# A one-core streaming encoder layer: softmax scores kept with their sign turned, softmax outputs ahead of older results, a bank of its own for turned v and y, and g_pre as one row spread by a product

## What is computed

```
proj = u @ w_in                      -> q, k, v of three attention branches
A: 4 heads, two maps each, T5 bias, causal by chunks of 64;
   w = softmax(map 0) - lam * softmax(map 1);  o = rmsnorm(w @ v, subln_g) * 0.8
B: 8 query heads over 2 shared k/v heads, a band of 2 chunks, T5 bias,
   and a sink term in the softmax's sum
C: 8 heads, a band of 9 chunks, relative bias
mixed = sum over branches of sigmoid(u @ w_gate + b_gate) * (y @ w_proj)
h = x + rmsnorm(mixed @ w_out, g_post_mix)
h = h + rmsnorm(conv_ffn(rmsnorm(h, g_pre_ffn)), g_post_ffn)
```

## Time and profile before

| | us |
|---|---|
| median of 3 runs (range) | 900.63 (898.75 to 901.16) |
| the profiled execution | 900.81 |
| its span, first to last instruction | 899.0 |
| TensorE busy | 875.3 |
| weight loads busy | 737.0 |
| GpSimd, VectorE, ScalarE busy | 455.3, 406.1, 397.4 |

### The profile page before, as it was taken

The page is one execution under the profiler, slowest core; times in us unless marked ns, Lnnn a source line. Parts: engine busy times, 40 slices in busy tenths (PEclk is TensorE's granted clock), DMA queues, the critical chain, the costliest instruction groups (busy, mean ns, idle before and its releaser), DMA issues.

```text
span 899.0 us, 13197 instructions
## 1 busy us (share of the span) xinstructions
PE 875.3 (97%) x4327; PEld 737.0 (82%) x4327; DVE 406.1 (45%) x889; ACT 397.4 (44%) x700; POOL 455.3 (51%) x622
## 2 busy tenths in 40 slices
PE   7999999999999999999999999999999999999997
PEld 6887888888888887888888889888888888888886
DVE  5678776666556652223222175444444444300004
ACT  5466566666655645333332245444444444311112
POOL 4453433324433327667766665555555555555551
PEclk9999999999999999999999999999999999999999
DMA  7442132332222212323335512333333332322202
GB/s 228 135 118 68 50 93 72 91 93 77 59 70 77 60 47 88 112 86 102 102 108 179 185 34 83 111 102 103 94 93 93 93 103 105 119 94 94 94 24 94
DMA packets 132141, 86.14 MB, mean 96 GB/s; under 512 B 6822, under 2 KB 121454, under 8 KB 132098
## 3 DMA queue, kind: packets, MB, share of 16 engines
q1 hardware_dynamic: 131050, 81.86, 30.4%
q10 hardware_dynamic: 1048, 3.72, 1.2%
HBM read 83.42 MB, written 2.14 MB: 95 GB/s over the span
## 4 chain that ended last, share of the span: by engine, by line
PE 86%; DVE 6%; ACT 3%; POOL 2%; issue 1%; DMA 1%; DVEq 0%; SPq 0%; POOLq 0%; ACTq 0%
PE banks L1237 27%; PE banks L1239 27%; PE banks L1238 27%; PE banks L1381 2%; POOL ring_lo L527 1%; PE banks L1310 1%; PE banks L1311 1%; DMA wide<-in_g_pre_mix_dram 1%; DVE scratch L1037 1%; PE banks L1256 1%; DVE pages L959 1%; DVE scratch L1066 1%; ACT pages L638 1%; DVE pages L954 0%; DVE pages L1000 0%
## 5 line engine op out<-in xcount | busy, mean ns | idle before, releaser
L527 POOL TENSOR_TENSOR ring_lo<-ring_raw,ring_hi 128x256 fp32r<-128x256 f32 x568 | 429.0, 789 | 394.3 <-ACT ring_hi L630 394.2
L1237 PE MATMUL banks<-u_hi,ring_hi 128*128 128x512 f32 (+1 forms) x800 | 309.8, 387 | 2.3 <-POOL ring_lo L527 1.7
L1239 PE MATMUL banks<-u_hi,ring_lo 128*128 128x512 f32 (+1 forms) x800 | 305.1, 381 | 0.0
L1238 PE MATMUL banks<-u_lo,ring_hi 128*128 128x512 f32 (+1 forms) x800 | 304.6, 381 | 0.0
L630 ACT CAST ring_hi<-ring_raw 128x1024 fp32r<-128x1024 f32 x142 | 147.8, 1043 | 134.6 <-PE banks L1239 126.3
L1237 PEld LDWEIGHTS banks<-u_hi,ring_hi 128*128 128x128 f32 x800 | 150.6, 188 | 30.4 <-POOL ring_lo L527 2.4
L1239 PEld LDWEIGHTS banks<-u_hi,ring_lo 128*128 128x128 f32 x800 | 150.4, 188 | 29.5
L1238 PEld LDWEIGHTS banks<-u_lo,ring_hi 128*128 128x128 f32 x800 | 150.7, 188 | 27.4
L1202 DVE SCALAR_TENSOR_TENSOR wide<-banks,cols,wide 128x511 f32<-128x511 f32 x88 | 65.9, 749 | 103.1 <-ACT wide L852 97.0
L1237 PE MATMUL banks<-ring_hi,pages 128*128 128x512 f32 x240 | 93.9, 391 | 0.1
L1238 PE MATMUL banks<-ring_lo,pages 128*128 128x512 f32 x240 | 93.4, 389 | 0.0
(11 more groups left out here) (137 smaller groups left out, 996.7 us busy)
## 6 DMA issues: line engine op xcount, KB each, us to landing
ring_raw<-in_w_ffn_up_dram SPq DMA_DIRECT2D x88, 256.0 KB, 3.2
ring_raw<-in_w_in_dram SPq DMA_DIRECT2D x60, 256.0 KB, 3.4
ring_raw<-in_w_gate_dram SPq DMA_DIRECT2D x48, 256.0 KB, 3.1
ring_raw<-in_w_ffn_down_dram SPq DMA_DIRECT2D x44, 256.0 KB, 2.8
ring_raw<-in_w_out_dram SPq DMA_DIRECT2D x16, 256.0 KB, 2.9
scratch<-in_x_dram SPq DMA_DIRECT2D x4, 512.0 KB, 6.2
ring_raw<-in_w_proj_a_dram SPq DMA_DIRECT2D x8, 256.0 KB, 2.8
ring_raw<-in_w_proj_c_dram SPq DMA_DIRECT2D x8, 256.0 KB, 3.1
```

Source lines behind the costliest of these rows:

```text
L527: last = pool.tensor_tensor(wlo[:, r, c], raw[:, r, c], whi[:, r, c].bitcast(F32), ALU.subtract)
L1237: pe.matmul(out, lhs_hi, rhs_hi, start=start, stop=False)
L1238: pe.matmul(out, lhs_hi, rhs_lo, start=False, stop=False)
L1239: return pe.matmul(out, lhs_lo, rhs_hi, start=False, stop=stop)
```

## The change

The scores are kept with their sign turned: the operation that adds the bias scales by -1 and takes the minimum, which is the negated maximum, so the negation goes; each exponential waits for its own map alone, and reads the scores with scale -1. B's sinks are negated once. On VectorE the head norm and the low parts of projections stay between `probs_low` and `softmax_out`, while `y_tok` and `y_low` go behind `softmax_out`; the reciprocals get a third buffer for it. `lam_ratio` is written as another operation. Turned v of units 0 to 3 and turned y of heads 0 to 2 go to bank 3, which A's probabilities don't use, and `turn_probs` waits for their low parts only from unit 4 on. At the start g_pre is loaded as one row on ScalarE's queue and spread to 128 partitions by two products with a row of ones, into banks 0 and 1, from where `xs` reads it; TensorE's warm-up is 10 transposes before these products, 10 behind them, and 16 behind the turning. ScalarE does `u_high(0)` ahead of `w_hi` of tile 0.

```diff
 SLOT_CUTS = {"A": (0, 5, 11, 17, 24), "C": (0, 5, 10, 16, 24), "B": (0, 6, 11, 17, 24)}
-WARM_UP = (28, 16)
+WARM_UP = (10, 10, 16)
...
         minus_half = sb("minus_half", [P, 4])
-        rowmax = sb("rowmax", [P, 2, 2])
+        neg_sink = sb("neg_sink", [P, PAIR_HEADS])
         negmax = sb("negmax", [P, 2, 2])
...
         sink_exp = sb("sink_exp", [P, 2, 2])
-        recip = sb("recip", [P, 2, 2])
+        recip = sb("recip", [P, 3, 2])
         lam_ratio = sb("lam_ratio", [P, 2])
...
         g_pre = wide[:, 2:4, :].rearrange("p h n -> p (h n)")
+        g_row, ones_row = g_pre[0:1, :], wide[0:1, 4, 0:P]
         xs_tmp = wide[:, 4:6, :].rearrange("p h n -> p (h n)")
...
+        def spread_gain():
...
+            return bank2(0)
...
         def turned_tokens(t, done):
...
             return (QK_PG + 2, K_LAST_PG)[group] + part
...
+        def turn_bank(u):
...
+            return PT_BANK + 1 if u < 4 else PT_BANK
...
             load_x(1)
-            sp.dma_start(g_pre, g_pre_mix[0].partition_broadcast(P)).then_inc(small_loaded[2], 16)
...
+            act.dma_start(g_row, g_pre_mix).then_inc(small_loaded[2], 16)
             act.wait_ge(x_loaded[0], 16)
...
             square(0, 1, x_tok[:, 1, :])
+            u_high(0, 0)
             w_hi_at(0)
-            u_high(0, 0)
             u_high(1, 0)
...
                 act.wait_ge(lam_done, 3)
-                act.activation(tiled(pages[:, Y_HI + u, :]), turned_rows(PT_BANK), ACT.Copy,
+                act.activation(tiled(pages[:, Y_HI + u, :]), turned_rows(turn_bank(u + 1)), ACT.Copy,
                                scale=sub_col[:]).then_inc(y_hi, 1)
...
                     probs_high(s - 1)
-                act.wait_ge(negmax_done, s + 1)
                 n = P * (qt + 1) if branch(u) != "B" else P + CHUNK * (qt > 0)
                 for m in range(2):
+                    act.wait_ge(biased, 2 * s + m + 1)
                     sp_m = scratch[:, P_PAGE + m, 0:n]
-                    act.activation(sp_m, sp_m, ACT.Exp, bias=negmax[:, s % 2, m:m + 1],
+                    act.activation(sp_m, sp_m, ACT.Exp, scale=-1.0, bias=negmax[:, s % 2, m:m + 1],
                                    accum_out=rowsum[:, s % 2, m:m + 1]).then_inc(exp_done, 1)
...
                         act.wait_ge(pv_done, TT * (u - 1))
-                    act.copy(pages[:, v_page(u, 0), :], psum[:, PT_BANK, :]).then_inc(v_hi, 1)
+                    act.copy(pages[:, v_page(u, 0), :], psum[:, turn_bank(u), :]).then_inc(v_hi, 1)
                 for t in split_now[1:]:
...
-            def xs(n, t, dst):
+            def xs(n, t, dst, gain=g_pre):
...
                 dve.scalar_tensor_tensor(out=dst, in0=x_tok[:, t, :], scalar=norm_rstd[:, n, t:t + 1],
-                                         in1=g_pre, op0=ALU.mult, op1=ALU.mult).then_inc(xs_done, 1)
+                                         in1=gain, op0=ALU.mult, op1=ALU.mult).then_inc(xs_done, 1)
...
+            dve.memset(ones_row, 1.0).then_inc(ones_set, 1)
             dve.memset(pages[CHUNK:P, QK_PG + 2:QK_PG + 8:5, :].bitcast(F32), 0.0).then_inc(q_lo_cleared, 1)
             dve.memset(pages[0:CHUNK, Q_LO_PG:Q_LO_PG + 2, :].bitcast(F32), 0.0).then_inc(q_lo_cleared, 1)
-            dve.wait_ge(small_loaded[2], 16)
+            dve.wait_ge(gain_spread, 1)
             for h in range(2):
                 for t in (2 * h, 2 * h + 1):
-                    xs(0, t, x_tok[:, t, :])
+                    xs(0, t, x_tok[:, t, :], spread_gain())
                 for t in (2 * h, 2 * h + 1):
...
                 dve.wait_ge(small_loaded[6], 16)
-                dve.wait_ge(lam_done, 3)
+                dve.tensor_scalar(neg_sink[:], sink[:], -1.0, None, ALU.mult).then_inc(lam_done, 1)
+                dve.wait_ge(lam_done, 4)
                 dve.wait_ge(mask_done, 1)
...
                 hi, lo = tiled(pages[:, Y_HI + u, :].bitcast(F32)), tiled(pages[:, Y_LO + u, :])
-                dve.scalar_tensor_tensor(out=lo, in0=turned_rows(PT_BANK), scalar=sub_col[:],
+                dve.scalar_tensor_tensor(out=lo, in0=turned_rows(turn_bank(u + 1)), scalar=sub_col[:],
                                          in1=hi, op0=ALU.mult, op1=sub).then_inc(y_lo, 1)
...
                     dve.wait_ge(y_turned, u - 1)
-                dve.tensor_scalar(dst, by_v_lo, recip[:, s % 2, 0:1], None, ALU.mult).then_inc(y_part, 1)
+                dve.tensor_scalar(dst, by_v_lo, recip[:, s % 3, 0:1], None, ALU.mult).then_inc(y_part, 1)
                 dve.wait_ge(y_part, s + 1)
-                dve.scalar_tensor_tensor(out=dst, in0=by_v_hi, scalar=recip[:, s % 2, 0:1], in1=dst,
+                dve.scalar_tensor_tensor(out=dst, in0=by_v_hi, scalar=recip[:, s % 3, 0:1], in1=dst,
                                          op0=ALU.mult, op1=ALU.add).then_inc(y_out, 1)
...
                         dve.wait_ge(mask_b_done, u - 7)
-                    floor = LOWEST if branch(u) != "B" else sink[:, 2 * (u - 8) + m:2 * (u - 8) + m + 1]
+                    ceiling = -LOWEST if branch(u) != "B" else neg_sink[:, 2 * (u - 8) + m:2 * (u - 8) + m + 1]
                     dve.tensor_tensor_reduce(scratch[:, P_PAGE + m, 0:n], psum[:, SC_BANK + m, 0:n],
-                                             scratch[:, BIAS_PAGE + b % 4, j0:j0 + n], 1.0, floor,
-                                             ALU.add, ALU.max, rowmax[:, s % 2, m:m + 1]).then_inc(biased, 1)
-                dve.wait_ge(biased, 2 * s + 2)
-                dve.tensor_scalar(negmax[:, s % 2, :], rowmax[:, s % 2, :], -1.0, None, ALU.mult)\
-                   .then_inc(negmax_done, 1)
+                                             scratch[:, BIAS_PAGE + b % 4, j0:j0 + n], -1.0, ceiling,
+                                             ALU.add, ALU.min, negmax[:, s % 2, m:m + 1]).then_inc(biased, 1)
                 if branch(u) == "B":
-                    dve.wait_ge(negmax_done, s + 1)
+                    dve.wait_ge(biased, 2 * s + 2)
                     dve.tensor_tensor(sink_arg[:, s % 2, :], sink[:, 2 * (u - 8):2 * (u - 8) + 2],
...
                     dve.wait_ge(sum_done, s - 32 + 1)
-                dve.reciprocal(recip[:, s % 2, :], rs).then_inc(recip_done, 1)
+                dve.reciprocal(recip[:, s % 3, :], rs).then_inc(recip_done, 1)
                 dve.wait_ge(recip_done, s + 1)
...
                     n = P * (qt + 1)
-                    dve.scalar_tensor_tensor(out=lam_ratio[:, s % 2:s % 2 + 1], in0=recip[:, s % 2, 1:2],
-                                             scalar=rs[:, 0:1], in1=neg_lam[:], op0=ALU.mult,
-                                             op1=ALU.mult).then_inc(ratio_done, 1)
+                    dve.tensor_scalar(lam_ratio[:, s % 2:s % 2 + 1], recip[:, s % 3, 1:2], rs[:, 0:1], neg_lam[:],
+                                      ALU.mult, ALU.mult).then_inc(ratio_done, 1)
                     dve.wait_ge(ratio_done, s + 1)
...
                         p_m = scratch[:, P_PAGE + m, 0:n]
-                        last = dve.tensor_scalar(p_m, p_m, recip[:, s % 2, m:m + 1], None, ALU.mult)
+                        last = dve.tensor_scalar(p_m, p_m, recip[:, s % 3, m:m + 1], None, ALU.mult)
                     last.then_inc(probs_ready, 1)
...
                     y_low(s - 1)
...
+            def normed_heads(s):
+                u, qt = divmod(s, TT)
                 if qt == 1 and 1 <= u <= 4:
...
                                       ALU.mult).then_inc(head_normed, 1)
...
+            def projections(s):
                 for g in range(3, T_ATT):
...
                     probs_low(s - 1)
+                    normed_heads(s - 1)
+                    projections(s - 1)
+                softmax_out(s)
+                if s >= 1:
                     results(s - 1)
-                softmax_out(s)
                 if qt == 0 and u <= 8:
                     dve.wait_ge(v_hi, u + 1)
-                    dve.tensor_tensor(pages[:, v_page(u, 1), :], psum[:, PT_BANK, :],
+                    dve.tensor_tensor(pages[:, v_page(u, 1), :], psum[:, turn_bank(u), :],
                                       pages[:, v_page(u, 0), :].bitcast(F32), sub).then_inc(v_lo, 1)
...
                 for _ in range(turns):
-                    pe.transpose(psum[:, 0, 0:P], ident[:], ident[:])
+                    pe.transpose(psum[:, 2, 0:P], ident[:], ident[:])
             keep_clock_up(WARM_UP[0])
+            pe.wait_ge(ones_set, 1)
+            pe.wait_ge(small_loaded[2], 16)
+            for h in range(2):
+                last = pe.matmul(psum[:, h, :], ones_row, g_row[:, 512 * h:512 * (h + 1)], start=True, stop=True)
+            last.then_inc(gain_spread, 1)
+            keep_clock_up(WARM_UP[1])
             for t in range(2):
                 turn_tokens(t, 0, x_tok[:, t, :])
-            keep_clock_up(WARM_UP[1])
+            keep_clock_up(WARM_UP[2])
...
                 pe.wait_ge(proj_act, [g for g, x in enumerate(TILES) if x == ("v", u)][0] + 1)
-                if u >= 1:
```

(22 more changed lines are left out.)

## The result

The changed kernel takes 890.82 us (median of 4 runs, 890.79 to 890.86) against 900.13 (4 runs, 898.75 to 901.16): ratio 0.9897, 95% interval 0.988 to 0.9915. It is 9.3 us faster; 13.2 was forecast, to 887.4. The profiled execution's span is 889.0 us.

A forecast was written before the change was run, and what follows sets the result against it. TensorE was taken as the bound, busy 875.3 of 899.0 us, leaving at most 23.7 open. Attention 11.3 plus start 1.9 gave 13.2, so 887.4 from the median 900.63; own range 885.5 to 890, wide range 884.5 to 892.5.

The forecast's parts named there:

- The start: Start of the kernel: g_pre as a row and two products bring tile 1 to 20.1 from 22.03, 1.9 us gained.
- the attention term: Slots of the attention part: four edits at the stalls of TensorE give 11.3 us, bounds 6 to 12.
- the wide range: Whole kernel: 884.5 to 892.5 us, the range that leaves out less than 2 in 10.
- I take the upper end: Start: both f32 products of g_pre's row priced at 0.9 to 1.6 us, with 1.6 taken.
- the second step: Start: u_high(0) ahead of w_hi has tile 0's split end at 14.55, using up the multiplication's gain and 0.4 more.
- the forecast's upper bound: Start: a gain of 2.9 us, with w_lo at 2.8.
- rival A: Start gives at most 1 us, by a later row or longer products; 888.8 us, chance 0.17.
- Own bank: Slots 0, 4, 6, 8, 10, 12, 14: a separate bank for turned v and y ends waits summing to 4.75 us.
- the 0.2 taken back: Slot 1: probabilities come only 0.5 to 0.8 earlier while TensorE comes 1.2 earlier, so 0.2 us is lost again.
- The order: Slots 3 to 45: y_tok and y_low behind softmax outputs; 2.16, 0.47, 0.8, 2.64 and 0.71 us, some with the negation.
- the forecast's 1.3 for both: Slots 3, 7, 11, 15: y_tok and the negation take 1.3 us out of VectorE's chain, ending stalls of 0.49 to 0.59.
- Rival B: Attention: another wait, ScalarE's casts before the exponentials, brings half the stalls back; 893 us, chance 0.14.

The follow-up runs named there:

- products_twice: The changed kernel with the two f32 products of g_pre's row made a second time: 894.75 us, ratio 0.9936 to the kernel before.
- no_middle_warm_up: The changed kernel with w_hi of tile 0 ahead of u_high(0) again and without the ten transposes behind g_pre's products: 889.21 us, ratio 0.9882.
- split_first: The changed kernel with ScalarE's w_hi of tile 0 ahead of u_high(0) again: 889.35 us, ratio 0.9886 to the kernel before.
- start_only: The kernel before with the edits of the start alone: 900.45 us, ratio 1.001 to the kernel before.
- attn_only: The changed kernel with the start of the kernel before: 890.88 us, ratio 0.9899 to the kernel before.
- bank_undone: The changed kernel with turned v and y in bank 2 for all units and the probabilities' turning waiting for their low parts: 894.19 us, ratio 0.9937.
- late_split: The changed kernel with the splits of weight tiles 29, 32, 35 and 38 one slot later: 888.88 us, ratio 0.9881 to the kernel before.
- broadcast_act: The changed kernel with w_hi of tile 0 first and g_pre's 512 KB broadcast on ScalarE's queue, without products: 892.51 us, ratio 0.9915.

## Why the prediction was right, and where its steps were off

**The direction, and where the time came from: right.** The attention part gave 9.58 us, within its bounds of 6 to 12 and under the 11.3 forecast. The waits left over stand at slots 16, 18, 31, 35, 39 and 43, as forecast (3.9 us for near 3), none at 0, 3 to 15 or 45, and what follows attention kept its length. The start gave 0.39 of its 1.9. So the profile's 10 us lack 1.7 us of the attention term and 1.5 of the start's. The medians differ by 9.3, since the profiled execution of the kernel before, 900.81, lies 0.7 above its median. The measured 890.82 lies inside the wide range and just outside the forecast's own 885.5 to 890.

**The start: the step that failed** is "I take the upper end", 1.6 us for both f32 products, and 1.9 us of gain with it. They take 3.8 (3.87 to 7.65), and `products_twice` repeats it (3.6). In reduced precision the pair takes 1.22 in the same stretch, so the f32 form costs three times that. TensorE's rate of the time may explain another part: the transposes ahead of and behind the products load weights every 0.20 us (10 in 2.00) against 0.11 behind 12.78 (16 in 1.78), though the granted clock reads 1.00 in both, and over the products too (window 4 to 8 us):

```profile
4.00:8.00 4.00, 4.00 (x6) 1.45 (x7) 0.32 (x1) 2.30 (x4) 1.50 (x4) 1.00 0.99 350
```

No run makes an f32 product later, so how much of the 3.8 is the early rate is not shown. The rule weighed in the prediction, four passes for a true f32 product in the Trainium skill ("FP8 and Floating Point Precision", TensorE Precision Notes), gave an estimate of 3.4 for both at 1.2 GHz, near the measured 3.8. At the 2.4 GHz that the record grants there, the same estimate is 1.7, so these runs bear the rule out only if the engine ran at the lower level, as the transposes' 0.20 suggests.

With the multiplication at 7.68, the second step fell too: that the swap of `u_high(0)` and `w_hi` of tile 0 costs next to nothing. The prediction had tile 0's split done at 14.55, ahead of u_low; it was done at 16.54 and TensorE waited 1.89 for it. Of these 2.0 us, 1.3 are the later multiplication. The other 0.7 are the ten warm-ups behind the products, a term that the prediction put at nothing: they held the turning of the tokens back to 9.76, and without them it began at 9.01 (`no_middle_warm_up`). `split_first` priced the swap at 1.5 us.

Tile 1 came at 21.30, for 20.1. That it came earlier than before at all was luck: its split on GpSimd took 2.83 where 3.78 was summed, which stood only in the forecast's upper bound (21.30 + 0.95 = 22.25 without it, for 22.03 before). Of the 0.73 gained there, the stretch up to the first scores gave 0.34 back, since the chain on VectorE did not move along as forecast: it reached the tables at 24.02, for 24.08 before, behind u_low of the later tokens, and the first scores waited for its end, k's low part. In the median of the runs nothing is left at all (`start_only`, `attn_only`), and `attn_only` shows an execution that turns the tokens faster with the start of before. So the start went as rival A has it, by a longer product and not by a later row.

**Own bank: right in place, over-sized.** Forecast 4.55 with the 0.2 taken back; 3.2 measured. Slot 0 gave 1.09 (1.18 forecast). Between the changed kernel and `bank_undone`, slots 4, 8 and 12 differ by 0.25 each, as forecast, and slots 6, 10 and 14 by 0.41 to 0.43, where 0.94 each was summed. (The 4.3 us expected of `bank_undone` had the same fault, with 0.7 for each of these slots.) The term that was off is reading the row of a weight load as the stall. In the changed kernel's slot 6, unstalled, the turning follows the last scores by 0.24:

```profile
75.83 0.40 PE L1333 MATMUL banks<-pages 128*128 128x512 f32 x1
76.07 0.49 PE L1411 MATMUL banks<-ident,scratch 128*128 128x128 f32 x3
```

Before, it followed them by 0.66, so TensorE lost 0.42 where the row says 0.67:

```profile
78.28 0.40 PE L1311 MATMUL banks<-pages 128*128 128x512 f32 x1
78.94 0.52 PE L1381 MATMUL banks<-ident,scratch 128*128 128x128 f32 x3 [0.26 <-DVE pages L992]
```

A weight load that runs ahead of its matmul waits longer than TensorE does.

**The order: right, over-sized at slots 31 to 43.** Forecast 6.78 for the order with the negation, which was to count in slots 3 to 15 alone. The order alone gave 4.1, the negation alone 0.8, and with the order undone slots 3, 7, 11, 15, 19 and 45 still gained 0.2 to 0.4 each. In the changed kernel slots 3, 7, 11, 15 gave 2.35 in all (forecast 2.16), slot 19 0.51 (0.47), slots 35, 39, 43 0.7 each (0.88), slot 45 0.7 (0.71), and slot 31 0.22 (0.8), 5.85 in all. The stalls of slots 3 to 15 were gone with the order alone; the forecast's 1.3 for both was more than they needed. The chain in slot 31 did move earlier, and so came to stand beside GpSimd's split: scalings of 1.78 us where they took 1.10 before. `late_split` shows that this is the cause: with 0.88 in place of 1.78, slot 31 gives 1.12. In slots 35, 39 and 43 the overlap was there before the change, so there it is not what the change lost but what it left: 0.55 in place of 1.26, and 0.6 us more from each. By slot 47 `late_split` has gained 2.4 us more.

**Rival B** did not come: ScalarE releases no turning of probabilities. The wait that did take over, in slot 31, was VectorE's own work slowed by GpSimd, which none of the rivals had.

## What to carry to other kernels

Price a true f32 product by a row or a test of its own before it goes on a path that sets the end: here 512 columns of one row cost 1.9 us, and 0.6 in reduced precision. When a chain on VectorE moves, look at what GpSimd does at its new time, as one would look at a queue. Undo each of two edits by itself before dividing a gain between them: here one paid for what the other had delayed. Read the size of a stall from the distance between matmuls, and only its place and cause from the weight load.

## What the runs showed of the hardware

- VectorE's work beside GpSimd's depends on where its operands are. Scalings from SBUF to SBUF take 1.26 us beside a split and 0.55 without, and GpSimd's split 3.78 beside multiplications with both operands in SBUF and 2.83 beside the same ones with an operand in PSUM (`18.33 2.83`); with the operand back in SBUF, in `broadcast_act`, it takes 3.77 again. This gained the changed kernel 0.95 us at tile 1.
- Transposes of the first 12 us of the changed kernel loaded weights every 0.20 us, against 0.11 later, while the granted clock read 1.00, so the record alone doesn't price the start.
- The same instructions at the start had the clock at 0.50 for the first products in two profiles, behind 2.39 us of idle time, and at 1.00 in others, behind 1.89 and 2.09; runs of one kernel lie 0.9 to 1.5 us apart.
